# Block 0 of an encoder's input projection: its third and fourth x tiles turned before they are scaled, their factors put on the products

## The reference

```python
def rmsnorm(x, g):
    r = lax.rsqrt(jnp.mean(xf * xf, axis=-1, keepdims=True) + EPS)
    return (xf * r * g).astype(x.dtype)

h = rmsnorm(x, norm1_g)
z = h @ w_in                      # 1024 x 1024
za, zb = z[..., :512], z[..., 512:]   # Fourier mixing | centred pooling
x = x + jnp.concatenate([fourier_mix(za), pool_mix(zb)], -1) @ w_out
x = x + (silu(norm(x) @ w_gate) * (norm(x) @ w_up)) @ w_down
```

## Time and profile before

| | |
|---|---|
| time, median of 3 runs | 2483.89 us (2483.2 to 2484.06) |
| the profiled execution, its own time | 2485.55 us |
| its span, first to last instruction | 2483.5 us |
| PE busy | 2466.7 us, 99% of the span |
| DVE, ACT, POOL busy | 1678.9, 941.7, 167.2 us |
| granted TensorE clock | 0.998 of full speed |

### The profile page before, as it was taken

One profiled execution on the slowest core, in us unless ns is written; L12 is line 12 of the kernel. 1 busy time (PEld: TensorE's weight loads), 2 busy tenths in 40 slices (PEclk: granted clock), 3 DMA queues, 4 the chain that ended last, 5 costly groups with the idle time before them and its releaser, 6 DMA issues.

```text
span 2483.5 us, 31738 instructions
## 1 busy us (share of the span) xinstructions
PE 2466.7 (99%) x11045; PEld 2040.3 (82%) x11045; DVE 1678.9 (68%) x2565; ACT 941.7 (38%) x1733; POOL 167.2 (7%) x222
## 2 busy tenths in 40 slices
PE   9999999999999999999999999999999999999998
PEld 7888878887888888888888888888888888888887
DVE  5555887898767767867677687676774464455565
ACT  5534476547333333433333333333332232233333
POOL 2555400000000000000000000000000000000000
PEclk9999999999999999999999999999999999999999
DMA  6433766787323223522232432222256654354554
GB/s 185 113 86 92 234 211 234 260 267 274 124 84 123 110 80 121 194 105 110 92 115 110 166 140 96 98 110 97 110 194 215 246 193 170 123 191 151 193 190 148
DMA packets 171944, 382.04 MB, mean 154 GB/s; under 512 B 13433, under 2 KB 71129, under 8 KB 162645
## 3 DMA queue, kind: packets, MB, share of 16 engines
q1 hardware_dynamic: 163184, 350.83, 41.4%
q0 software_dynamic: 8240, 29.94, 3.2%
q10 hardware_dynamic: 432, 0.14, 0.0%
HBM read 254.24 MB, written 126.62 MB: 153 GB/s over the span
## 4 chain that ended last, share of the span: by engine, by line
PE 86%; DVE 1%; ACT 0%; DMA 0%; issue 0%; DVEq 0%; ACTq 0%
PE bank L352 29%; PE bank L354 29%; PE bank L353 28%; DMA a_raw<-ha_scr 0%; PE bank L2091 0%; PE bank L1377 0%; DVE a_lo L2685 0%; PE bank L1063 0%; ACT a_hi L2493 0%; DVE zy_late L1048 0%; DVE scratch L1037 0%; DVE scratch L1040 0%; DVE uv_lo L1075 0%; DVE wm_lo L1289 0%; ACT xn L1667 0%
## 5 line engine op out<-in xcount | busy, mean ns | idle before, releaser
L352 PE MATMUL bank<-a_hi,w_hi 128*128 128x512 f32 x1848 | 720.2, 390 | 3.5 <-DVE w_lo L2708 3.4
L354 PE MATMUL bank<-a_hi,w_lo 128*128 128x512 f32 x1848 | 719.5, 389 | 0.0
L353 PE MATMUL bank<-a_lo,w_hi 128*128 128x512 f32 x1672 | 650.9, 389 | 0.0
L352 PEld LDWEIGHTS bank<-a_hi,w_hi 128*128 128x128 f32 x1848 | 347.2, 188 | 78.0 <-DVE w_lo L2708 4.3
L354 PEld LDWEIGHTS bank<-a_hi,w_lo 128*128 128x128 f32 x1848 | 347.1, 188 | 72.3
L353 PEld LDWEIGHTS bank<-a_lo,w_hi 128*128 128x128 f32 x1672 | 314.2, 188 | 65.0
L352 PE MATMUL bank<-t_hi,s_hi 128*128 128x512 f32 x924 | 359.4, 389 | 0.0
L353 PE MATMUL bank<-t_lo,s_hi 128*128 128x512 f32 x924 | 359.4, 389 | 0.0
L354 PE MATMUL bank<-t_hi,s_lo 128*128 128x512 f32 x924 | 359.4, 389 | 0.0
L2506 ACT ACTIVATE w_hi<-t_raw 128x512 fp32r<-128x512 f32 x256 | 162.1, 633 | 462.0 <-PE bank L354 378.4
L2860 DVE TENSOR_TENSOR s_lo<-s_raw,s_hi 128x512 fp32r<-128x512 f32 x231 | 156.0, 686 | 231.1 <-ACT s_hi L2581 231.1
(11 more groups left out here) (284 smaller groups left out, 3216.7 us busy)
## 6 DMA issues: line engine op xcount, KB each, us to landing
s_scr<-sums_out SPq DMA_DIRECT2D x33, 1792.0 KB, 5.9
s_raw<-s_scr SPq DMA_DIRECT2D x42, 1024.0 KB, 5.0
w_raw<-in_w_gate SPq DMA_DIRECT2D x64, 512.0 KB, 3.6
w_raw<-in_w_up SPq DMA_DIRECT2D x64, 512.0 KB, 4.4
wd_staged<-in_w_down SPq DMA_DIRECT2D x121, 256.0 KB
a_raw<-ha_scr SPq DMA_DIRECT2D x21, 1024.0 KB, 5.4
s_raw<-s_scr SPq DMA_DIRECT2D x21, 768.0 KB, 4.3
x<-in_x SPq DMA_DIRECT2D x24, 512.0 KB, 5.9
```

The costliest lines, as they stand in the source:

```text
L352: pe.matmul(out, w_hi, m_hi, start=first, stop=False, **checks)
L353: pe.matmul(out, w_hi, m_lo, start=False, stop=False, **checks)
L354: return pe.matmul(out, w_lo, m_hi, start=False, stop=last, **checks)
```

## The change

Block 0's tiles 2 and 3 are no longer scaled. PE turns them as soon as they have landed, and z's columns 256 to 511 (their tokens) carry no factor when they leave PSUM. The 256 factors are written by SP to a scratch row in DRAM and read back to all partitions (`rstd_row`). DVE multiplies the right half of each z tile by that row as it leaves PSUM (`first_scaled`), eleven operations in all, and ACT copies only the left half, after DVE's half is there. Tiles 0 and 1 are scaled on DVE (left side) and later on ACT (right side). Around this, several steps move: the four warm-up matmuls ahead of the gain are gone and six follow it; DVE turns the gain first of all; DVE rounds the first row of w; the second root comes between the rows; four of block 1's squares go behind `stage_z(0, 0)`; two quarters of block 1's scaling instead of one are ACT's; `junk` is used in two pieces instead of four.

```diff
+        sp.wait_ge(const_or_rstd_moved, DMA)
+        sp.wait_ge(rstd_chain, 2 * 4)
+        sp.dma_start(rstd_scr.rearrange("(t p) -> p t", p=P), rstd[:, 0, 2:4], allow_slow_non_contiguous=True
+                     ).then_inc(const_or_rstd_moved, DMA)
+        sp.wait_ge(const_or_rstd_moved, 2 * DMA)
+        sp.dma_start(rstd_row[:, :], rstd_scr.partition_broadcast(P)).then_inc(const_or_rstd_moved, DMA)
         sp.wait_ge(transposed, KT)
         load_x(2, 0)
...
         def stage_z(j, c, first=False):
+            cols = slice(0, HALF // 2) if first else slice(0, HALF)
             act.wait_ge(z_ready, j * KT + c + 1)
+            if first:
+                act.wait_ge(left_or_z_scaled, 2 + c + 1)
...
         first_squares()
-        for d in range(KT):
+        act.wait_ge(constants_made, GAIN_MADE)
+        round_h(0, 0, 0, first=True)
+        round_h(0, 0, 1, first=True)
+        act.wait_ge(w_hi_done, 1)
+        for d in range(1, KT):
             act.wait_ge(ahead.row_loaded[d], DMA)
             act.activation(w_hi[:, POOLED, d, :], ...).then_inc(w_hi_done, 1)
-            if d == 0:
-                act.wait_ge(rstd_chain, 2 * 4)
-                for side, done in ((slice(0, HALF), left_scaled), (slice(HALF, D), xn_ready)):
-                    act.activation(xin[0][:, 2, side], ..., scale=rstd[:, 0, 2:3]).then_inc(done, 1)
-                act.wait_ge(constants_made, GAIN_MADE)
-            round_h(0, 0, d, first=True)
-            if d == 6:
-                squares(1, 2 * ROWS * DMA, 1, range(4))
+            if d == 1:
+                for t in range(2):
+                    act.activation(xin[0][:, t, HALF:], ..., scale=rstd[:, 0, t:t + 1]).then_inc(xn_ready, 1)
+            else:
+                round_h(0, 0, d, first=True)
+            if d == 3:
+                first_root(1)
         stage_z(0, 0, first=True)
+        squares(1, 2 * ROWS * DMA, 1, range(4))
...
-        for b in range(12, NBLK):
+        for b in range(8, NBLK):
...
+        def first_scaled(c):
+            right = slice(HALF // 2, HALF)
+            dve.wait_ge(z_ready, c + 1)
+            if c == 0:
+                dve.wait_ge(const_or_rstd_moved, 3 * DMA)
+            if c >= HEADS:
+                h = c - HEADS
+                if h >= 2:
+                    dve.wait_ge(z_stored[h - 2], DMA)
+                scaled = dve.tensor_tensor(z_out[:, h % 2, right], z_ps[c % 4][:, right], rstd_row[:, :], ALU.mult)
+            else:
+                scaled = dve.tensor_tensor(zb[:, c, ...], z_ps[c][:, right], rstd_row[:, :], ALU.mult)
+                if c:
+                    scaled = dve.scalar_tensor_tensor(out=zk[:, c - 1, ...], in0=z_ps[c][:, right], ...)
+            scaled.then_inc(left_or_z_scaled, 1)
...
         copy_turned(0)
         for k in range(KT):
             if k + 1 < KT:
                 copy_turned(k + 1)
+            if k == 0:
+                for c in range(HEADS):
+                    first_scaled(c)
             rest_of_folded(k)
-        step(0, 0, quarters=3)
+        first_step()
...
+        def first_step():
+            norm(1, 1, quarters=2)
+            first_scaled(HEADS)
+            for d in range(3):
+                turn(1, 1, d)
+            for d in range(KT):
+                if d in (2, 4, 6):
+                    first_scaled(HEADS + d // 2)
+                rest_of_h(1, 1, d)
+                if d + 3 < KT:
+                    turn(1, 1, d + 3)
...
-        warm_up(4)
...
-        warm_up(5)
-        for t in range(2):
-            pe.wait_ge(xn_ready, t + 1)
-            for d in range(4):
-                pe.transpose(t_ps[d][:, t * P:(t + 1) * P], every_fourth(xin[0][:, t, :], d), eye[:, :])
-        warm_up(2)
-        pe.wait_ge(left_scaled, 2)
-        for d in range(4):
-            for t in range(2, 4):
-                mm = pe.transpose(...)
-            mm.then_inc(transposed, 1)
-        warm_up(2)
+        pe.wait_ge(x_first[0], DMA)
+        warm_up(6)
+        pe.wait_ge(x_first[2], DMA)
+        for d in range(4):
+            turn_tile(2, d)
+        pe.wait_ge(x_first[3], DMA)
+        turn_tile(3, 0)
+        turn_tile(3, 1)
+        for d in range(2):
+            for t in range(2):
+                if d == 0:
+                    pe.wait_ge(left_or_z_scaled, t + 1)
+                mm = turn_tile(t, d)
+            mm.then_inc(transposed, 1)
+        for d in range(2, 4):
+            for t in (3, 0, 1):
+                mm = turn_tile(t, d)
+            mm.then_inc(transposed, 1)
```

More of the change, by code:

```diff
@@ L372, in every_fourth, with project_in @@
     return ap.rearrange("p (s j r) -> p s r j", s=2, r=ROWS)[:, d // ROWS, d % ROWS]
-def project_in(nc, ctx, ahead, mixer, pooled, x, w_in, g1, ident, z_scr, table, channel, edge):
+def project_in(nc, ctx, ahead, mixer, pooled, x, w_in, g1, ident, z_scr, rstd_scr, table, channel, edge):
     NJ = TOKENS // HALF
@@ L612, in vector, with rows_variance, rows_inverse @@
     def vector(dve):
-        def rows_norm(tiles, count, squares):
-            dve.wait_ge(squares_done, squares)
+        def rows_variance(half):
+            tiles = slice(2 * half, 2 * half + 2)
+            dve.wait_ge(squares_done, 2 * half + 2)
             dve.tensor_scalar(var[:, 0, tiles], sumsq[:, 0, tiles], 1.0 / D, EPS, ALU.mult, ALU.add).then_inc(var_ready, 1)
-            dve.wait_ge(std_ready, count + 1)
-            refined_rstd(dve, rstd_chain, count * 4, std[:, 0, tiles], var[:, 0, tiles], tmp[:, 0, tiles], rstd[:, 0, tiles])
+        def rows_inverse(half):
+            tiles = slice(2 * half, 2 * half + 2)
+            dve.wait_ge(std_ready, half + 1)
+            refined_rstd(dve, rstd_chain, half * 4, std[:, 0, tiles], var[:, 0, tiles], tmp[:, 0, tiles], rstd[:, 0, tiles])
+        def first_scaled(c):
[9 more added lines that the diff above has]
+            else:
+                scaled = dve.tensor_tensor(zb[:, c, 2 * PAD + HALF // 2:2 * PAD + HALF], z_ps[c][:, right], rstd_row[:, :],
+                                           ALU.mult)
+                if c:
+                    scaled = dve.scalar_tensor_tensor(out=zk[:, c - 1, PAD + HALF // 2:PAD + HALF], in0=z_ps[c][:, right],
+                                                      scalar=float(WINDOWS[c]), in1=rstd_row[:, :], op0=ALU.mult, op1=ALU.mult)
+            scaled.then_inc(left_or_z_scaled, 1)
         def norm(j, slot, quarters=4):
@@ L681, in vector @@
                             ).then_inc(constants_made, 1)
+        rows_variance(0)
+        rows_inverse(0)
+        for t in range(2):
+            dve.tensor_scalar(xin[0][:, t, 0:HALF], xin[0][:, t, 0:HALF], rstd[:, 0, t:t + 1], None,
+                              ALU.mult).then_inc(left_or_z_scaled, 1)
+        dve.wait_ge(ahead.row_loaded[0], DMA)
+        dve.tensor_copy(w_hi[:, POOLED, 0, :], w_raw[:, 0, HALF:].rearrange("p (g e) -> p g e", g=4)).then_inc(w_hi_done, 1)
         dve.wait_ge(constants_made, GAIN_MADE)
@@ L714, in transposes @@
             if d == 4:
-                pe.wait_ge(xn_ready, 4)
+                pe.wait_ge(xn_ready, 2)
             if d >= 4:
@@ L3138, in encoder @@
         pooled = Pooled(ahead, y_scr)
-        front = project_in(nc, ctx, ahead, mixer, pooled, x, w_in, g1, ident, z_scr, table, channel, edge)
+        front = project_in(nc, ctx, ahead, mixer, pooled, x, w_in, g1, ident, z_scr, rstd_scr, table, channel, edge)
         mixing = mix(nc, ctx, ahead, mixer, z_scr, y_scr, w_pool)
```

61 lines of the change are left out of this document (33 added, 28 removed).

## The result

The changed kernel takes 2494.32 us (median of 6 runs, 2493.55 to 2495.68), the kernel before on the same chip 2484.06. The ratio is 1.0040, 95% interval 1.0030 to 1.0051: slower by 10.3 us, where +2.0 us was forecast and 2488.2 was the upper end of the range.

A forecast was written before the change was run, and what follows sets the result against it. PE, busy 99% of the span, was taken as the bound. The start's 0.76 us gain is used up and 2.0 lost at the hand-over: 2483.89 + 2.0 = 2485.9 us, range 2483.0 to 2488.2.

The forecast's parts named there:

- The start: Up to the first product: it comes 0.85 us earlier, at 12.7 instead of 13.56.
- row 6 of w: PE's wait for this row's load, there at 29.21 regardless, cuts the start's gain to 0.76 us.
- The factor row: Trip through DRAM before the folds: lands at 34.2, bounds 33.1 to 39.3, costing 0 if landed by 36.3.
- Queued behind, only the last part counts: Factor row's write in SP's queue: lands at 31.2, behind the edge table's 30.6; bounds 30.6 and 34.7.
- rival 2: Factor row late at the folds: PE loses one for one from 36.3, plus 2.8 at the hand-over; chance 0.13.
- the hand-over: Block 0 to block 1: VectorE delivers late to PE; 0.76 used up and 2.0 us lost, bounds +0.3 to +2.8.
- 13.2 + 4.4 + 1.7: VectorE's chain at the hand-over: turns and rests 13.2 us, three first_scaled rounds 4.4, GpSimd's part 1.7.
- 0.05 for slower by over 0.2%: Whole kernel: chance 0.05 of being slower by more than 0.2% (5 us), which needs the late factor row.
- Rivals 1, 3 and 4: Gain stays at hand-over: 2483.1, chance 0.14; clock rises later: 2487.0, 0.08; start no earlier: 2486.7, 0.05.
- Rival 3: At the start PE's clock rises 3 us later: shift +0.3, total +3.1, 2487.0 us; chance 0.08.

The follow-up runs named there:

- e4_act_trip: Changed kernel with both DMAs of the factor row issued from ScalarE's queue instead of SP's; 2495.73 us.
- e5: Changed kernel with 22 matmuls on zeros in front of PE's wait at the folds, the row still late; 2492.02 us.
- e6: Changed kernel writing 8-byte pieces and reading 128 different rows of x instead of the scratch row, some factors left out; one run, 2489.57 us.
- e7: Changed kernel with SP waiting for the factor row's read before issuing block 2's x; one run, 6.6 us more than the kernel before.
- e1: Changed kernel with the factor row made by PE transposes and a ScalarE copy instead of the trip through DRAM; 2488.04 us.
- e8: Changed kernel with factors written as one 8-byte run per partition, VectorE reading them with a stride, all computed; 2488.14 us.

## Why the prediction was wrong

- *The start*: right, 12.78 for the first product (12.7 forecast). That 0.76 us are left at row 6 of w is luck: in the changed kernel row 6 came at 27.7 instead of 29.2 and did not bind, and the gain was 0.78 from the start, set by PE's own transposes. In the repeat of it the row came at 29.4, PE waited 0.67 us there, and 0.41 us were left at the folds.
- *The factor row*: the step that failed, a cost taken as 0. I took 0.6 us from the edge table's landing to the write's and 2.5 for the read; they were 4.4 and 6.5. The upper bound of the write (34.7) was just what it took; that of the read (4.1) was too low, since none of the rows it came from read one KB 128 times, nor one just written, nor did I count the x pieces, which the change itself puts right behind the read. The row landed at 41.3, outside the bounds of 33.1 to 39.3. "Queued behind, only the last part counts" held for pieces of 8 bytes (0.15 us behind the edge table) and not for pieces of 4.
- *What a late row costs*: rival 2 had the mechanism, with its deciding point, a landing at 36.3, and one for one beyond: 41.3 - 36.3 = 5.0, and 5.04 were measured. Its sum for 41.3, +4.2 for the shift and 2.8 for the hand-over, gives +7.0. Missing were 2.2 us for the clock, which I had weighed only for the first matmuls and not for an idle time later on, 0.5 at the hand-over and 0.4 behind it.
- *The hand-over*: right in mechanism, nearly right in size. The three idle times of VectorE (1.12, 1.11, 1.11) and the length of the whole chain (66.13 to 85.37, 19.2 us; 13.2 + 4.4 + 1.7 = 19.3 forecast) are as worked out. PE lost 3.29 instead of 2.8, because the chain began later than I had put it: 1/rms was to be there 1.7 us earlier than before with PE's own 0.76 in it, 0.9 without; it came 0.4 earlier, since the operation at 61.09 took 1.24 us for 0.81 beside GpSimd. The last start adds 0.1: row 7 follows row 6 by 0.80 us, not 0.69.
- *Chances*: 0.05 for slower by over 0.2% was too small. The two trips in series stood in the text with no row for either of their forms, and the upper ends of their bounds were treated as unlikely rather than as unknown.
- *Rivals 1, 3 and 4*: no. VectorE's gain at the root (1/rms at 62.79, where 56.77 + 6.45 = 63.2 would be level with PE) didn't save the hand-over, and the start came sooner. Rival 3 came true in small: PE's transposes are still 0.21 us apart until 12.2 us, where those of the kernel before are 0.12 apart from 11.93 on, so the clock seems to have risen later; but not by the 3 us that would have made the start late.

## What to carry to other kernels

When an operand moves to the other side of a product, count the new way by which it gets there, in the form that the DMA really has: how many pieces, how small, and whether all read the same bytes; if no row shows that form, the bound is open and belongs into the range. Where a wait is put into one in-order queue, look for what the next operation of the waiting engine needs from that same queue: VectorE, ScalarE and VectorE one after the other cost 1.1 us each time, and moving the calls one or two rows ahead cut the loss from 3.3 to 0.6 us. Price an idle time of PE with the clock that may be lost behind it, also where it comes in several short pieces. And where differences are as small as these, compare where PE stands in the traces, stage by stage, and not the ends.

## What the runs showed of the hardware

- A write of 256 pieces of 4 bytes landed 4.4 us after the DMA ahead of it in its queue; 128 pieces of 8 bytes landed 0.15 us after it. From another queue, issued beside loads of 200 to 400 GB/s, the write of 4-byte pieces took 13.6 us and a row of w that came at 27.7 to 29.4 in the other traces came at 34.0.
- 128 partitions reading the same 1 KB, written just before: 4.0 us alone, 4.8 to 6.5 with other loads behind it in its queue, 8.0 from ScalarE's queue beside SyncE's loads; 128 different KB of x: 2.0 us.
- After PE had stood idle for 5.4 (e4_act_trip), 5.1, 3.9 and 3.7 us the clock was granted at 0.50 for a while, right after 1.6 us it wasn't; behind 5.1 us that cost 2.2 to 2.4 us on top of the idle time, behind 3.9 and 3.7 us 1.6.
- Idle times of 0.56, 0.66 and 1.24 us, within 4.5 us of each other at the hand-over, were followed by a clock of 0.50 for 3.4 us in the traces of e4, e5, e6 and e7, and not in those of the changed kernel, its repeat, e1 and e8. It cost about 1.4 us where it came.
- A VectorE operation on 16 columns with two SBUF tensors took 0.17 us with GpSimd idle and 0.81 to 1.25 beside a GpSimd product, ending when that product ended.
- VectorE reading PSUM and SBUF took 0.38 to 0.41 us for 256 columns, GpSimd at work or not, while rests with two SBUF inputs took 0.70 to 1.69.
- PE turned one column, read with stride zero, into a row on all partitions, two times 128 columns in 0.38 us.
